# The opening of a two-block transformer kernel on one core: plain x transposed, norm weights put in later, high products first

## The reference, cut to what matters

```python
def rms_norm(x, g):
    x32 = x.astype(jnp.float32)
    y = x32 * lax.rsqrt(jnp.mean(x32 * x32, axis=-1, keepdims=True) + EPS)
    return (y * g.astype(jnp.float32)).astype(x.dtype)

h = rms_norm(x, g[0])
m = neighborhood_attention(h, na_w_qkv[j], na_rpb[j], na_w_o[j])   # qkv = h @ w_qkv, 16 heads of 64
...
lam_full = exp(sum(lam32[0] * lam32[1])) - exp(sum(lam32[2] * lam32[3])) + lambda_init   # layer 2
...
ang = positions.astype(jnp.float32)[..., None] * inv_freq        # rotary angles, second block
cos, sin = jnp.cos(ang), jnp.sin(ang)
```

## Time and profile before

| | us |
|---|---|
| median of 3 runs | 1222.5 (1222.41 to 1223.94) |
| the profiled execution | 1221.93 |
| its span in the profile | 1220.2 |
| PE busy in the span | 1205.2 (99%) |
| DVE busy | 944.3 (77%) |
| ACT busy | 672.7 (55%) |

### The profile page before, as it was taken

One profiled execution on the slowest core, in us unless ns is written; L12 is line 12 of the kernel. 1 busy time (PEld: TensorE's weight loads), 2 busy tenths in 40 slices (PEclk: granted clock), 3 DMA queues, 4 the chain that ended last, 5 costly groups with the idle time before them and its releaser, 6 DMA issues.

```text
span 1220.2 us, 17906 instructions
## 1 busy us (share of the span) xinstructions
PE 1205.2 (99%) x6995; PEld 1052.0 (86%) x6995; DVE 944.3 (77%) x1270; ACT 672.7 (55%) x1064; POOL 139.3 (11%) x257
## 2 busy tenths in 40 slices
PE   8999999999999999999999999999999999999997
PEld 7899888888879888888888988888897888888886
DVE  6757699888876588998888898766776868667665
ACT  6656644434576777444446845443586655444445
POOL 4000330000120012000001200000207420000002
PEclk9999999999999999999999999999999999999999
DMA  8834376565445445665564575566455136665540
GB/s 271 243 124 155 105 253 204 190 207 182 164 155 173 139 133 176 212 204 181 191 208 138 188 249 173 187 195 198 145 174 172 36 126 215 203 206 176 201 143 35
DMA packets 149015, 214.52 MB, mean 176 GB/s; under 512 B 4410, under 2 KB 114428, under 8 KB 148932
## 3 DMA queue, kind: packets, MB, share of 16 engines
q1 hardware_dynamic: 145596, 205.39, 51.1%
q0 software_dynamic: 1632, 4.71, 1.4%
q10 hardware_dynamic: 1704, 3.28, 0.8%
HBM read 212.30 MB, written 1.06 MB: 175 GB/s over the span
## 4 chain that ended last, share of the span: by engine, by line
PE 92%; DVE 5%; ACT 2%; issue 1%; POOL 0%; DMA 0%; POOLq 0%; ACTq 0%; DVEq 0%
PE work L2349 24%; PE work L2352 12%; PE acc L1948 10%; PE acc L1949 10%; PE acc L1950 9%; PE work L1948 5%; PE work L1949 5%; PE work L1950 5%; PE work L2158 2%; PE work L1970 2%; DVE w_lo L1263 2%; PE acc L2134 1%; PE work L2338 1%; PE work L2326 1%; PE work L2340 1%; PE work L2467 1%
## 5 line engine op out<-in xcount | busy, mean ns | idle before, releaser
L1263 DVE TENSOR_TENSOR w_lo<-raw,w_hi 128x2048 fp32r<-128x2048 f32 (+1 forms) x194 | 439.9, 2274 | 50.7 <-ACT w_hi L695 50.7
L695 ACT ACTIVATE w_hi<-raw 128x2048 fp32r<-128x2048 f32 (+2 forms) x193 | 365.2, 1899 | 68.8 <-PE work L2352 59.8
L2349 PE MATMUL work<-hT_both,w_hi 128*128 128x512 f32 x1280 | 318.8, 391 | 0.0
L2349 PEld LDWEIGHTS work<-hT_both,w_hi 128*128 128x128 f32 x1280 | 234.8, 188 | 45.2
L2352 PEld LDWEIGHTS work<-hT_both,w_lo 128*128 128x128 f32 x1280 | 174.6, 190 | 12.5
L2352 PE MATMUL work<-hT_both,w_lo 128*128 128x256 f32 x1280 | 178.5, 282 | 0.0
L1948 PE MATMUL acc<-w_hi,aux_hi 128*128 128x512 f32 x400 | 157.8, 395 | 0.0
L1949 PE MATMUL acc<-w_lo,aux_hi 128*128 128x512 f32 x400 | 156.7, 392 | 0.0
L1950 PE MATMUL acc<-w_hi,aux_lo 128*128 128x512 f32 x400 | 155.8, 389 | 0.0
L1050 ACT ACTIVATE aux_hi<-Z 128x256 fp32r<-128x256 f32 x88 | 36.9, 419 | 195.1 <-DVE Z L1673 107.1
L1644 DVE TENSOR_REDUCE Z<-work 128x256 f32<-128x512 f32 x88 | 60.5, 688 | 90.4 <-PE work L2352 88.7
(11 more groups left out here) (262 smaller groups left out, 1807.2 us busy)
## 6 DMA issues: line engine op xcount, KB each, us to landing
raw<-in_ffn_w_in SPq DMA_DIRECT2D x44, 1024.0 KB, 5.1
raw<-in_ffn_w_out SPq DMA_DIRECT2D x22, 1024.0 KB, 5.1
raw<-in_w_gate SPq DMA_DIRECT2D x22, 1024.0 KB, 5.3
raw<-in_w_up SPq DMA_DIRECT2D x22, 1024.0 KB, 5.3
raw<-in_w_down SPq DMA_DIRECT2D x22, 1024.0 KB, 5.0
raw<-in_na_w_qkv SPq DMA_DIRECT2D x12, 1024.0 KB, 7.3
raw<-in_da_w_qkv SPq DMA_DIRECT2D x12, 1024.0 KB, 5.4
raw<-in_ple_w_gate SPq DMA_DIRECT2D x8, 1024.0 KB, 5.1
```

The source lines that it names most:

```text
L695: act.activation(w_hi[:, n % RING, 0:size], raw[:, n % RAW, 0:size], ACT.Copy).then_inc(hi_done, 1)
L1263: dve.tensor_tensor(w_lo[:, n % RING, 0:size], raw[:, n % RAW, 0:size], w_hi[:, n % RING, 0:size].bitcast(F32), ALU.subtract).then_inc(lo_ ...
L2349: pe.matmul(b.rearrange("p (e s) -> p e s", e=2), v[0][:, k, cols(c % 2)], hT_both[:, k, :, :], start=k == 0, stop=False)
```

## The change

In phase 0, x is transposed as it is loaded, in 16 blocks straight into the four `acc` banks (`turn_first`), both token tiles of a block side by side, so that one ACT and one DVE instruction of 128x256 make the high and the low part, with the norm weight as the scale. Phase 0 joins `UNSCALED`: the reciprocal root of each token is multiplied in when columns are read out. That reading moves from ACT to DVE (`column_scaled`, 16 instructions of 128x256 that replace the 16 `columns_out` of ACT); values are scaled in ACT's copy of them. The sums of squares come after the high parts on ACT.

Slab 0 is loaded in two halves, and POOL and DVE split it in halves. PE makes all high products of slab 0 and then its low ones, and does slab 1 in the same manner (`first_columns(n)`), with `turn_scales(0)` between. The first value columns and the transposed constants then stand ahead of the first scores. `keep_busy` falls from 25 matmuls in four places to 12 in three.

On DVE the low part of slab 3 comes ahead of the first scores, that of slab 4 ahead of the second scores as before; on ACT the high parts of slabs 3 and 4 both come ahead of the first exponentials. `lambdas` moves behind the first scores, `rotary` to a place between the readings of columns c6 and c7, and the sine on ACT into phase 3, before that phase's first exponentials. The loads of lambda, positions and table move from ACT's queue to POOL's, behind `rpb`; the load of the gains (`gb`, 512 KB) moves from the opening to a place behind the transposed weights of unit 3. `expand(1)` precedes the first scores.

The columns are gone from ACT there, two table loads with them, and one more slab stands ahead of each unit's exponentials. The diff, cut to its core:

```diff
-UNSCALED = [1, 4, 6, 7, 8]
+UNSCALED = [0, 1, 4, 6, 7, 8]
+SCALED_OUT = [1, 4]
...
+        def first_block(k):
+            return acc[:, k % 4, k // 4 * S:(k // 4 + 1) * S]
...
-                sp.dma_start(raw[:, n % RAW, 0:k * c].rearrange("p (k n) -> p k n", k=k), src)\
-                    .then_inc(landed[n % RAW], 16)
+                dst = raw[:, n % RAW, 0:k * c].rearrange("p (k n) -> p k n", k=k)
+                if n == 0:
+                    sp.dma_start(dst[:, 0:4, :], src[:, 0:4, :]).then_inc(first_half, 16)
+                    sp.dma_start(dst[:, 4:8, :], src[:, 4:8, :]).then_inc(landed[0], 16)
+                else:
+                    sp.dma_start(dst, src).then_inc(landed[n % RAW], 16)
             for i, (t, q) in enumerate(((0, 0), (0, 1), (1, 1))):
...
-            powers("pre0.1")
-            pool.wait_ge(landed[0], 16)
-            pool.tensor_copy(w_hi[:, 0, :], raw[:, 0, :]).then_inc(hi_done, 1)
             for i in range(32):
                 ins = pool.memset(invf[:, i:i + 1], float(np.float32(10000.0) ** np.float32(-i / 32)))
             ins.then_inc(freq_ready, 1)
-            pool.wait_ge(hi_done, 2)
+            first, second = slice(0, SLAB // 2), slice(SLAB // 2, SLAB)
+            pool.wait_ge(first_half, 16)
+            pool.tensor_copy(w_hi[:, 0, first], raw[:, 0, first]).then_inc(first_hi, 1)
+            pool.wait_ge(landed[0], 16)
+            pool.tensor_copy(w_hi[:, 0, second], raw[:, 0, second]).then_inc(hi_done, 1)
+            powers("pre0.1")
             load_rpb(0)
+            pool.dma_start(z(11864, 12120), bass.AP(w["da_lambda"].tensor, 0, [[0, P], [1, 256]])).then_inc(lam_loaded, 16)
+            with nc.allow_non_contiguous_dma(reason="256 positions and 256 table entries, once"):
+                pool.dma_start(posi[:, :], w["positions_2"][0].rearrange("(t p) -> p t", p=P)).then_inc(pos_loaded, 16)
+                pool.dma_start(tT[:, :], w["t5_table"].rearrange("b h -> h b")).then_inc(t5_loaded, 16)
             link(pool.memset(wmask[:, :], 0.0))
...
-                g = G[f"v{ph}.{half}.{t}"]
-                evac(g, vtok[:, t, half * 512:(half + 1) * 512], bank(g))
+                g, dst = G[f"v{ph}.{half}.{t}"], vtok[:, t, half * 512:(half + 1) * 512]
+                if ph == 0:
+                    i, c = E[f"pre0.{t}"]
+                    full(act, g)
+                    act.wait_ge(rstd_done, i + 1)
+                    act.activation(dst, bank(g), ACT.Copy, scale=rstd[:, c:c + 1]).then_inc(bank_free[g % WORK], 1)
+                else:
+                    evac(g, dst, bank(g))
 
...
             def attention0():
                 b = B[0]
-                columns_out(0, 2)
-                columns_out(0, 3)
-                feed(b + 4)
+                feed(b + 5)
                 unit_exps(0, 0)
-                feed(b + 5)
+                act.wait_ge(lam_sum, 1)
+                act.activation(lame[:, :], lamc[:, 0:2], ACT.Exp).then_inc(lam_exp, 1)
+                feed(b + 6)
                 unit_exps(0, 1)
                 weights_turned(0, 0)
                 values_out(0, 0, 0)
                 values_out(0, 0, 1)
...
+                act.wait_ge(rot_ready, 1)
+                angles = trig[:, :, :, :].rearrange("p a b c -> p (a b c)")
+                act.activation(angles, angles, ACT.Sin).then_inc(trig_ready, 1)
...
             act.dma_start(vrow[0:KT, :], rows[0][0].rearrange("(r p) -> r p", p=P)).then_inc(first_row, 16)
-            for t in range(T):
-                pre(0, t)
-            act.dma_start(z(11864, 12120), bass.AP(w["da_lambda"].tensor, 0, [[0, P], [1, 256]])).then_inc(lam_loaded, 16)
-            with nc.allow_non_contiguous_dma(reason="256 positions and 256 table entries, once"):
-                act.dma_start(posi[:, :], w["positions_2"][0].rearrange("(t p) -> p t", p=P)).then_inc(pos_loaded, 16)
-                act.dma_start(tT[:, :], w["t5_table"].rearrange("b h -> h b")).then_inc(t5_loaded, 16)
-            gains(w["norm_g"][0, 1], D)
-
+            act.wait_ge(ident_ready, 1)
+            table(ACT.Exp)
             evacuated(act, G["vec"])
-            tile_parts(0, 0)
-            tile_parts(0, 1)
+            for k in range(KT):
+                if k < 4:
+                    act.wait_ge(turn_full, k + 1)
+                else:
+                    act.wait_ge(part_ready, k - 3)
+                split(hT_hi[:, k, :], first_block(k), gains_of(0, k))
+            pre(0, 0)
+            pre(0, 1)
             act.wait_ge(hi_done, 1)
             fed[0] = 1
             feed(3)
-            columns_out(0, 0)
-            columns_out(0, 1)
-            act.wait_ge(rot_ready, 1)
-            act.activation(trig[:, :, :, :].rearrange("p a b c -> p (a b c)"), rot, ACT.Sin).then_inc(trig_ready, 1)
-            act.wait_ge(lam_sum, 1)
-            act.activation(lame[:, :], lamc[:, 0:2], ACT.Exp).then_inc(lam_exp, 1)
+            scales_out(0)
...
+            def column_scaled(n):
+                g, f = G[f"c0.{n}"], n // 4 * 2 + n % 2
+                if n == 0:
+                    dve.wait_ge(scales_ready, UNSCALED.index(0) + 1)
+                full(dve, g)
+                src, roots = [v.rearrange("p (t c) -> p t c", t=T) for v in (bank(g)[:, 0:S], rb0)]
+                dst = (kT if n // 2 % 2 else qT)[:, f, :].rearrange("p (t c) -> p t c", t=T)
+                dve.tensor_tensor(dst if n // 2 % 2 else backwards(dst), src, roots, ALU.mult)\
+                    .then_inc(bank_free[g % WORK], 1)
+
             def attention0():
                 b = B[0]
                 feed(b + 3)
+                for n in range(4):
+                    column_scaled(n)
                 expand(0)
+                feed(b + 4)
+                expand(1)
                 scores(0, 0)
-                expand(1)
+                lambdas()
                 taps_out()
-                feed(b + 4)
+                feed(b + 5)
                 scores(0, 1)
                 expand(2)
-                feed(b + 5)
+                feed(b + 6)
+                column_scaled(4)
                 expand(3)
-                feed(b + 6)
                 feed(b + 7)
+                dve.wait_ge(lam_exp, 1)
+                link(dve.tensor_tensor(lamc[:, 2:3], lame[:, 1:2], lame[:, 0:1], ALU.subtract))
+                dve.tensor_scalar(lamc[:, 3:4], lamc[:, 2:3], LAMBDA_INIT, None, ALU.subtract)
                 output(0)
+                feed(b + 8)
+                column_scaled(5)
                 output(1)
-                feed(b + 8)
                 feed(b + 9)
+                column_scaled(6)
+                rotary()
+                column_scaled(7)
...
+            for k in range(KT):
+                split(hT_lo[:, k, :], first_block(k), hT_hi[:, k, :], k + 1, gains_of(0, k))
+            first, second = slices(SLAB // 2)
+            dve.wait_ge(first_hi, 1)
+            dve.tensor_tensor(w_lo[:, 0, first], raw[:, 0, first], w_hi[:, 0, first].bitcast(F32), ALU.subtract)
+            dve.wait_ge(hi_done, 1)
+            dve.tensor_tensor(w_lo[:, 0, second], raw[:, 0, second], w_hi[:, 0, second].bitcast(F32), ALU.subtract)\
+                .then_inc(lo_done, 1)
+            fed[0] = 1
             feed(2)
-            lambdas()
-            rotary()
...
+            def turn_first():
+                for t in range(T):
+                    pe.wait_ge(x_loaded[t], 16)
+                    for i in range(4):
+                        for k in (i, i + 4):
+                            ins = pe.transpose(first_block(k)[:, cols(t)], x[:, t, cols(k)], ident[:, :])
+                        if t == 1:
+                            ins.then_inc(turn_full, 1)
...
-            def first_columns():
-                v = w_hi[:, 0, :].rearrange("p (k n) -> p k n", k=KT)
-                pe.wait_ge(hi_done, 1)
+            def first_columns(n):
+                hi, b = w_hi[:, n, :].rearrange("p (k n) -> p k n", k=KT), []
                 for c in range(2):
-                    b = open_bank(pe, G[f"c0.{c}"])
-                    for k in BLOCKS:
-                        if c == 0:
-                            split_done(pe, 0, 1, k)
-                        for part in (hT_hi, hT_lo):
-                            pe.matmul(b[:, 0:S], v[:, k, cols(c)], part[:, k, :], start=k == 0 and part is hT_hi, stop=False)
-                v = slab(0)[1]
+                    b.append(open_bank(pe, G[f"c0.{2 * n + c}"])[:, 0:S])
+                if n:
+                    pe.wait_ge(hi_done, n + 1)
+                for k in range(KT):
+                    if n == 0:
+                        split_done(pe, 0, 1, k)
+                        if k == 0:
+                            pe.wait_ge(first_hi, 1)
+                        if k == 4:
+                            pe.wait_ge(hi_done, 1)
+                    for c in range(2):
+                        pe.matmul(b[c], hi[:, k, cols(c)], hT_hi[:, k, :], start=k == 0, stop=False)
```

(31 more changed lines are left out.)

48 lines of the change are left out of this document (20 added, 28 removed).

## The result

The changed kernel takes **1230.12 us** (median of six runs, 1226.33 to 1231.22) against 1222.47 (median of six, 1222.27 to 1223.94): ratio 1.0054, 95% interval 1.0042 to 1.0066. The forecast was 1221.0 with a range of 1218.0 to 1223.6, so the result is outside it and on the other side: the change costs 0.5% where a gain was expected. The profiled run of the changed kernel took 1230.16 with a span of 1228.4, 8.2 us above the span before.

What follows compares the result with a forecast made beforehand. PE bounds the kernel; its opening lead of 5.3 us, less a wait of 3.9 ahead of c4 (start 40.1 instead of 41.58), leaves 1.5 us gained: median 1221.0 against 1222.5, range 1218.0 to 1223.6.

Steps and rivals of the forecast that it cites:

- What bounds the kernel, and the yardstick c4: PE, busy 1205.2 of 1220.2 us; the gain is 41.58 less column c4's new start, if no later wait comes.
- The opening: Phase 0 on PE: slab 0 high products 8.4 to 12.3, low ones to 14.2, v0.0 opened at 21.3; 5.3 us early.
- The rule against the opening: Transposes don't count as busy array; with a low clock slab 0's high products cost 3.9 more, leaving gain 0.8.
- POOL's three small instructions, "about 1.1": Second root on POOL takes about 1.1 us behind the last square at 11.4, so rpb is issued at 12.5.
- I take 23.0, since its row is of the same two transfers: Landing of rpb and slab 3: 2.26 MB from 14.2 at 258 GB/s, 8.8 us, ending at 23.0.
- The bounds of 20.7 and 24.3: Limits for slab 3's landing: 20.7 at the 348 to 353 GB/s of slabs alone, 24.3 at the lowest slice, 224.
- slab 3 comes late: Rival, chance 0.09: landing at 24.5 loses the gain; at 26, perhaps with slab 4 behind, c4 starts at 43.1, time 1225.8.
- The chain of 15.1 us: From DVE's start on slab 3's low part, through unit 1's exponentials and ACT's bank readings, to c4: 15.1 us.
- A wait of 3.9 at c4: PE ready at 36.2 waits 3.9 us for ACT's reading of v0.0; c4 starts at 40.1, leaving 1.5 gained.
- The clock in the new wait: Rival, chance 0.12: the granted clock falls in PE's wait ahead of c4, costing 1.8; gain -0.3, time 1222.8.
- What was costed at nothing: Column readings (6.7 us) and rotary (3.7) on DVE, the sine in phase 3, small loads on POOL: all covered.
- The whole lead kept: Rival, chance 0.05: v0.0 read by 36, slab 3 landed by 19; gain 5.3 us, time 1217.2.

Runs made afterwards that it cites:

- the last run above: Changed kernel with rpb halved and ahead of the roots, ACT's three readings ahead of unit 1's exponentials, and keep_busy(4) instead of keep_busy(2) at the start: 1216.88 us (0.9955).

## Why the prediction was wrong, point by point

- **What bounds the kernel, and the yardstick c4**: right. The new waits all lie ahead of c4, and 5.56 of the 8.2 us is its later start.
- **The opening**: the mechanism was right, the size 1.0 us too hopeful. High products ran 9.70 to 13.5 (8.4 to 12.3 forecast), low ones ended at 15.7 (14.2), v0.0 opened at 22.3 (21.3). The term that was mis-sized is the first transposed pair: ACT's first high part began at 7.6, not at 6.3, as the 16 transposes (5.17 to 8.6) ran 0.21 apart at the 1.2 GHz level; with them at the fast pace it began at 6.73 (the last run above). DVE's eight low parts followed 1.3 late, to 11.4, and behind them slab 0's low part, which ended at 13.69 and held the low products. The high products started late also because the six `keep_busy` matmuls stood ahead of them until 9.9; this cost nothing, since the low ones waited for DVE.
- **The rule against the opening** (a transpose doesn't count as a busy array: the Trainium skill, TensorE: Matmul & The Clock Gate, Part 4: PE-mode transpose): the cold high products that it would have given did not come; they stood 0.12 apart in every run here. The granted clock rose at 8.3 us, while the transposes ran, and in other runs with the new opening between 5.9 and 9.7. Whether the transposes counted towards it no run shows, since `keep_busy` matmuls ran ahead of them and behind them.
- **POOL's three small instructions, "about 1.1"**: this is the first step that failed. `rpb` was issued at 20.14, not at 12.5. Of these 7.6 us 1.7 are the squares, which ended at 13.13, not at 11.4. The rest is POOL: it was still at the first root until 14.80 (1.7 more), and the three instructions of the second took from 14.90 to 20.19 (4.2 more than 1.1), as DVE's low parts held those that read SBUF. In the kernel before the roots ran while DVE was idle but for a short copy and 6.97 to 7.85; I took a length from there without asking what DVE would be doing in the new place.
- **"I take 23.0, since its row is of the same two transfers"**: the second step that failed, and on its own. With `rpb` issued at 13.3, slab 3 landed at 26.5. The larger part is a term that was left out, the other transfers in the queues by then: 2.90 MB came from 14.2 us on, not 2.26. The smaller part is the rate, 236 GB/s instead of the 258 of the earlier trace rows, which were a mean over another stretch. (With `rpb` issued at 10.3 it was 2.93 MB from 14.0 to 26.75, and the rate was down to 172 to 186 for 8 us.) The bounds of 20.7 and 24.3 didn't hold it either. The rival "slab 3 comes late" named the threshold (24.5) and the companion (slab 4); it had a chance of 0.09. Its landing at 26 is that of the run with `rpb` at 13.3, and its time, 1225.8 against 1225.6, is in part luck: it had a wait of 7 us and 1.8 for the clock, the run a wait of 4.03 and 1.5 (c4's block took 4.44). It is not the case of the changed kernel, where slab 3 landed early.
- **The chain of 15.1 us**: right, 15.21 to 15.22 in four runs.
- **A wait of 3.9 at c4**: 4.0, by coincidence. PE came later too, held by a wait of 3.6 for slab 3 that wasn't foreseen, because DVE's list puts the bias table of `rpb` ahead of slab 3's low part. I had written that "`rpb` itself allows it earlier", and with that dropped the one transfer that decided.
- **The clock in the new wait**: it had 0.12 and a price of 1.8. It fell with both waits and cost 2.3 to 2.4, once. The same page of the Trainium skill, "Why this matters for your kernels", warns of pauses between matmuls; the rows at 0.50 agree.
- **What was costed at nothing** (column readings on DVE, the rotary preparation, the sine in phase 3, the small loads on POOL): right for the time. PE shows no wait between c4 and 160 us, and in phase 3 the same ones as before. The bank masks on POOL were ready at 25.3, not near 19; that hid behind DVE's wait for `rpb`, and where half of `rpb` came first DVE waited 0.81 us for them, at no cost to PE.
- **The whole lead kept** (1217.2, chance 0.05): not what the change does, but what the kernel with half of `rpb` first does, 1217.47.

## What to carry to other kernels

When an instruction is moved, its length in the old place is a fact about the old place: look at what the engine that shares its port does at the new time, and at what is queued behind it. A DMA issue that stood behind six tiny computations cost 2.5 us here (1230.12 against 1227.59). A lead of the busiest engine is worth only as much as the chain that starts at the next landing lets through, so measure from that landing to the point of use first, and cut what must land by then (half of a table was enough). When a landing is worked out from bytes and a rate, count every transfer that will be issued before it lands, and take the rate as one of that mixture only.
